# Query weights: conversions of pieces 6 and 7 moved ahead of copies, lower parts moved ahead of the first dots

## What is computed

```python
def peer_ffn(xn, w_query, subkeys, u_tab, v_tab):
    q = (xt @ w_query).reshape(T, PEER_HEADS, 2, PEER_QDIM // 2)
    s = jnp.einsum('thpd,hpkd->thpk', q, subkeys)
    sv, si = lax.top_k(s, PEER_TOPK)
    ...
    top_s, pos = lax.top_k(cand, PEER_TOPK)
    expert = jnp.take_along_axis(cand_id, pos, axis=-1)
    gate = jax.nn.softmax(top_s, axis=-1)
    ...
        act = jax.nn.gelu(jnp.einsum('thkd,td->thk', u_tab[ec], xc), approximate=False)
        return jnp.einsum('thk,thkd->td', gc * act, v_tab[ec])
```

## Time and profile before

| | |
|---|---|
| median of 3 runs | 1543.56 us (1541.64 to 1547.15) |
| profiled execution | 1545.37 us, of which 1543.6 us are the span of the trace |
| TensorE busy | 1382.1 us (90%) |
| VectorE busy | 1030.1 us (67%) |
| ScalarE busy | 710.3 us (46%) |
| GpSimd busy | 562.7 us (36%) |
| DMA | 414.99 MB, mean 269 GB/s |

### The profile page before, as it was taken

One profiled execution on the slowest core, in us unless ns is written; L12 is line 12 of the kernel. 1 busy time (PEld: TensorE's weight loads), 2 busy tenths in 40 slices (PEclk: granted clock), 3 DMA queues, 4 the chain that ended last, 5 costly groups with the idle time before them and its releaser, 6 DMA issues.

```text
span 1543.6 us, 18198 instructions
## 1 busy us (share of the span) xinstructions
PE 1382.1 (90%) x5969; PEld 969.5 (63%) x5969; DVE 1030.1 (67%) x1918; ACT 710.3 (46%) x1377; POOL 562.7 (36%) x537
## 2 busy tenths in 40 slices
PE   7999998778877877787888999999999999999998
PEld 5887963333333332333335878788888778888887
DVE  5885687666666666666655548569863586498734
ACT  5545553322223333322324463377645755776534
POOL 3031454333333433333342422045443512364414
PEclk9999999999999899999898999899999999999999
DMA  9295699999999999999997510557664443476650
GB/s 314 92 181 184 248 389 421 421 422 421 422 422 422 421 422 422 421 422 421 422 420 274 191 51 10 164 165 216 190 218 175 163 139 104 126 208 194 215 190 28
DMA packets 180739, 414.99 MB, mean 269 GB/s; under 512 B 9178, under 2 KB 113218, under 8 KB 148418
## 3 DMA queue, kind: packets, MB, share of 16 engines
q0 software_dynamic: 37440, 268.45, 41.9%
q1 hardware_dynamic: 143090, 145.66, 30.7%
q10 hardware_dynamic: 144, 0.04, 0.0%
HBM read 409.93 MB, written 4.19 MB: 268 GB/s over the span
## 4 chain that ended last, share of the span: by engine, by line
PE 52%; DMA 24%; DVE 8%; ACT 6%; POOL 5%; issue 4%; ACTq 0%; POOLq 0%; DVEq 0%
DMA expert_rows<-in_peer_uv,route_idx 16%; PE ps L2515 9%; PE ps L2062 8%; PE ps L2064 8%; PE ps L2063 8%; PE ps L2346 8%; DMA work_b<-in_peer_uv,route_idx 6%; PE ps L2516 5%; POOL expert_rows L637 2%; POOL weights_lo L588 2%; DVE weights_lo L440 2%; DMA work_b<-in_peer_u,route_idx 2%; ACT weights_hi L433 2%; PE ps L2027 1%; POOL ple_proj_lo L588 1%
## 5 line engine op out<-in xcount | busy, mean ns | idle before, releaser
L1643 DVE CUSTOM_DVE_ANT_0 expert_rows<-expert_rows,ps 128x1024 f32<-128x1024 f32 x180 | 219.5, 1220 | 134.6 <-DMA expert_rows<-in_peer_uv,route_idx 133.3
L2346 PE MATMUL ps<-expert_rows,proj 128*128 128x512 f32 x512 | 247.6, 641 | 61.6 <-ACT proj L951 61.6
L637 POOL DMA_INDIRECT expert_rows<-in_peer_uv,route_idx x191 | 182.9, 958 | 285.1 <-PE ps L2346 215.1
L588 POOL TENSOR_TENSOR weights_lo<-weights_raw,weights_hi 128x512 fp32r<-128x512 f32 x112 | 147.1, 1348 | 365.7 <-ACT weights_hi L433 291.6
L433 ACT CAST weights_hi<-weights_raw 128x2048 fp32r<-128x2048 f32 x98 | 185.4, 1916 | 104.9 <-PE ps L2064 84.9
L2346 PEld LDWEIGHTS ps<-expert_rows,proj 128*128 128x128 f32 x512 | 102.6, 205 | 205.7 <-issue 122.1
L2515 PE MATMUL ps<-x_normT,weights_hi 128*128 128x512 f32 x640 | 222.5, 392 | 0.0
L440 DVE TENSOR_TENSOR weights_lo<-weights_raw,weights_hi 128x2048 fp32r<-128x2048 f32 x70 | 165.1, 2367 | 64.0 <-ACT weights_hi L433 63.6
L937 ACT ACTIVATE proj<-proj 128x4 f32<-128x4 f32 x64 | 13.1, 205 | 411.5 <-DVE proj L1643 411.5
L2062 PE MATMUL ps<-weights_hi,x_normT 128*128 128x512 f32 (+1 forms) x496 | 189.9, 383 | 12.6 <-DVE weights_lo L440 6.5
L2064 PE MATMUL ps<-weights_hi,x_normT 128*128 128x512 f32 (+1 forms) x496 | 186.6, 376 | 0.0
(11 more groups left out here) (367 smaller groups left out, 2407.1 us busy)
## 6 DMA issues: line engine op xcount, KB each, us to landing
weights_raw<-in_ffn_up SPq DMA_DIRECT2D x88, 512.0 KB, 5.0
weights_raw<-in_ffn_down SPq DMA_DIRECT2D x22, 1024.0 KB, 4.9
weights_raw<-in_ab_w_in SPq DMA_DIRECT2D x14, 1024.0 KB, 5.2
weights_raw<-in_w_in SPq DMA_DIRECT2D x12, 1024.0 KB, 7.9
weights_raw<-in_ple_gate SPq DMA_DIRECT2D x8, 1024.0 KB, 6.7
weights_raw<-in_c_w_in SPq DMA_DIRECT2D x6, 1024.0 KB, 5.7
weights_raw<-in_w_out SPq DMA_DIRECT2D x4, 1024.0 KB, 11.9
weights_raw<-in_peer_w_query SPq DMA_DIRECT2D x4, 1024.0 KB, 11.9
```

The source lines that it names most:

```text
L588: ins = pool.tensor_tensor(w.lo[:, c], w.raw[:, c], w.hi[:, c].bitcast(F32), ALU.subtract)
L637: nc.gpsimd.indirect_dma_start(out=dst, out_offset=None, in_=table, in_offset=bass.IndirectOffsetOnAxis(ap=r_idx[:, q, n:n + 1], axis=0)). ...
L1643: ins = nc.vector.tensor_tensor_reduce(out=rows, in0=rows, in1=tokens, scale=1.0, scalar=0.0, op0=ALU.mult, op1=ALU.add, accum_out=r_dot[: ...
L2346: ins = pe.matmul(PS[:, (J[f"peer_{t}"] + m) % 8, :], DIAG[b][:, k, :], rows[:, m * BANK:(m + 1) * BANK], start=False, stop=False, skip_gr ...
```

## The change

ScalarE's list: the conversion of piece 6 goes ahead of the copy of product 3, and that of piece 7 ahead of the copies of products 4 and 5. VectorE's list: the lower parts of pieces 6 and 7 go ahead of the first block's dots.

```diff
@@ scalar
             query_cols(1)
             query_cols(0)
-            for n in range(4, 8):
+            split("query", 4)
+            query_cols(2)
+            for n in range(5, 7):
                 split("query", n)
-                query_cols(n - 2)
+            query_cols(3)
+            split("query", 7)
+            for m in range(4, 6):
+                query_cols(m)
             weights(0, 0, 0)
             diag(0, 0, wait=False)
             query_cols(6)
@@ vector
-            for n in range(4, 6):
+            for n in range(4, 8):
                 split_lo(v, "query", n)
             v.wait_ge(sem("tokens_scaled"), 1)
             first_dots(0)
-            for n in range(6, 8):
-                split_lo(v, "query", n)
             route_stages(1, 1, range(14))
             first_dots(1)
```

## The result

| | before | changed |
|---|---|---|
| median of 20 runs | 1545.49 us (1541.14 to 1547.66) | 1549.34 us (1547.71 to 1550.93) |
| profiled execution | 1545.37 us, span 1543.6 | 1550.93 us, span 1549.1 |

The ratio is 1.0027, with a 95% interval of 1.0019 to 1.0035. The medians differ by 3.85 us where +2.2 was forecast. The point estimate is inside the 0.3% that count as no change, but the interval is clear of 1. Part of the distance to 1545.8 is the base: the three runs shown before had a median of 1543.56, the twenty have 1545.49. The profiled execution of the changed kernel was the slowest of its twenty.

What follows compares the result with a forecast made beforehand. From about 197 to 820 us a DMA stream of 1 MB gathers was taken to set the time. Score delay 2.6 plus clock 1.7 less free slip 2.1 gave +2.2 us, 1545.8 from 1543.56; range 1541.5 to 1549.0.

Steps and rivals of the forecast that it cites:

- ScalarE: moved, but not earlier: Conversions of pieces 6 and 7 still wait for TensorE's products and stay at 184.85 and 190.61 us; price 0.
- VectorE's lower parts: Piece 6's lower part and gather 6 come 1.1 us sooner, piece 7's and gather 7 stay; gain 0, at best 1.1.
- The dots of block 0: On VectorE they move to 194.82 to 199.4 us, later work slips 4.6 us, VectorE catches up; cost nothing.
- What waits for those dots: ScalarE's weights and copies 6 and 7 wait; scores, gather 13 and unit 1's first gather come 2.6 us later.
- The clock: TensorE's gap among the scores may bring slow matmuls costing 0, 1.7 or 2.9 us more; 1.7 taken.
- What of it reaches the stream: Unit 1's first gather can be issued 2.1 us later for nothing, since the queue was full; sum +2.2 us.
- An unknown: gathers issued under dots: Gather 7 and unit 1's first gather, issued on GpSimd beside VectorE's dots, may each take nothing or 1.0 us longer.
- Gather 13 has more room and does not come into it: Gather 13, moved from 208.56 to 211.2 us, was held to add nothing to the stream's delay.

Runs made afterwards that it cites:

- e1: The kernel before with only ScalarE's half of the change, VectorE as before: 1546.28 us, ratio 1.0003.
- e2: The kernel before with only VectorE's half of the change, ScalarE as before: 1549.19 us, ratio 1.0025.
- e3: The changed kernel, but ScalarE copies products 6 and 7 ahead of block 0's weights: 1545.61 us, ratio 1.0000 to the kernel before.
- e4_slip24: The kernel before with 24 small unread copies on ScalarE ahead of the copy of product 7: 1547.21 us, ratio 1.0009.
- e8: The changed kernel without the four zero matmuls that open the first half's sums: 1546.55 us, ratio 1.0014 to the kernel before.
- e6: Changed kernel with unit 1's routing ahead of block 0's dots on VectorE, and block 0's weights later on ScalarE: 1544.62 us, 0.9987 to the kernel before.
- e9: Changed kernel with copies 6 and 7 ahead of block 0's weights, gather 8 early, no zero matmuls before the first sum: 1544.97 us, 0.9995 to the kernel before.
- r_before: The kernel before, unchanged, run once more for a second trace: ratio 1.0006.
- r_after: The changed kernel run once more for a second trace: ratio 1.0025 to the kernel before.
- e7b: Repeat of e7, the same kernel: 1541.96 us, ratio 0.9986 to the kernel before.
- e5: The kernel before with gather 8 issued ahead of gathers 6 and 7: 1546.67 us, ratio 1.0005.
- the three e4: The kernel before with 12, 17 or 24 small unread copies on ScalarE ahead of the copy of product 7: 1543.70, 1545.07 and 1547.21 us.
- e7: The kernel before with gather 8 issued early and without the four zero matmuls that open the first half's sums: 1542.87 us, ratio 0.9990.

## Why the prediction was wrong

Point by point, by its own steps.

- **ScalarE: moved, but not earlier** was right: conversions in place, e1 1.0003.
- **VectorE's lower parts** was right: gather 6 at 191.08 (189.95 without the 1.13; forecast 189.9), gather 7 at 27.59 us behind the first gather, 27.56 before.
- **The dots of block 0** was right on VectorE: 195.97 less 1.13 is 194.84. That it could catch up was right as well, though its last dot is 1.3 us later than before, since gather 15 landed later.
- **What waits for those dots** was right to 0.2 us: gap 2.43 us (forecast 2.6), copy 7 at 205.65 (206.78 less 1.13; forecast 205.8), unit 1's first gather 2.7 us late (forecast 2.6). e2 and e3 show the path.
- **The clock** was taken at 1.7 us. In both profiles of the changed kernel it cost 0. In e2, e4_slip24 and e8 it cost 1.4 to 1.6.
- **The failed step is "What of it reaches the stream"**: "Its issue can therefore slip 7.6 - 5.5 = 2.1 us for nothing". The last dot of unit 1 came 3.5 and 3.3 us later for an issue 2.7 us later, and unit 15's 2.1 and 2.7 us: nothing was free, and without that term the forecast's 2.6 would have stood between the two. With the clock held, the forecast's own sum was 2.6 + 0 - 2.1 = +0.5. That it said +2.2 is owed to a clock term that did not come; two errors of 2 us cancelled.
- **An unknown: gathers issued under dots** was right that they can be lengthened: gather 8 took 1.99 us under block 0's dots, and 0.94 in e6, where no dots run beside it. It cost nothing at gathers 7 and 8 (e3, e9). The Trainium skill (SBUF — State Buffer, section "Who interferes with whom") infers that generating descriptors is not held up by a VectorE instruction with two SBUF inputs. These runs speak against that for this gather: the dots are the one thing that e6 moves away. The gather also reads its row numbers from SBUF (`route_idx`), so whether its reading or its descriptors waited is not shown.

What the prediction did not see is that the hold-up goes either way. The same dot and the same gather 15, a row of VectorE's timeline and one of GpSimd's, in the kernel before and then in r_before:

```profile
212.04 1.21 DVE L1643 CUSTOM_DVE_ANT_0 expert_rows<-expert_rows,x_norm 128x1024 f32<-128x1024 f32 x1
212.08 1.98 POOL L637 DMA_INDIRECT work_b<-in_peer_uv,route_idx  x1 [0.30 <-issue]
```

```profile
212.03 1.29 DVE L1643 CUSTOM_DVE_ANT_0 expert_rows<-expert_rows,x_norm 128x1024 f32<-128x1024 f32 x1
212.07 0.94 POOL L637 DMA_INDIRECT work_b<-in_peer_uv,route_idx  x1 [0.30 <-issue]
```

Either the gather takes 1 us more or the dot 0.08 us more. Of the first twenty gathers in each of the 16 profiles, 32 begin 0.02 to 0.1 us behind the start of such a dot: 25 took 1.97 to 1.99 us beside a dot of 1.21 to 1.23, and 7 took 0.93 to 0.94 us beside a dot of 1.28 to 1.30.

Why the slip was not free: the landing of one gather was taken for the state of the queue. Gather 7's 5.5 us (when it was issued, gather 6 had 1.0 us to go: 190.98 + 5.7) say how soon one gather lands, not when the next ones do. The rows of the kernel before already gave less. Gather 8, 1.25 us behind gather 7, and unit 1's second gather, 1.24 us behind its first, us from issue to landing:

```profile
scratch<-in_peer_uv,route_idx POOLq DMA_INDIRECT x1, 7.5
```

```profile
expert_rows<-in_peer_uv,route_idx POOLq DMA_INDIRECT x1, 8.8
```

At the second landing only 8.8 - 7.5 = 1.3 us are to be had, not 2.1. e4_slip24 bears this out: its second gather took 7.5 us too and landed 3.0 us late (62.5 against 59.6, counted from the first gather), which is 4.29 - 1.3. In r_after the same working gives 1.4 us, and the second gather was 3.1 us late, as late as the first, after 1.3 us at gather 15 (landed at 55.9 against 54.6). So it explains e4_slip24, but only a part of the change. Gather 13 was issued 2.7 us late too, and "Gather 13 has more room and does not come into it" was the second half of the mistake: between gathers 12 and 13 no gather was issued for 6.63 us instead of 3.07, and some 3 us behind gather 13's issue the rate sagged (351 and then 332 GB/s above) while the engines looked busy. That the low rate comes from few gathers in the queue is read from the place of the sags; no run varied the depth of the queue alone.

**What stays open.** The last dot of unit 15 is 2.1 and 2.7 us later, the medians differ by 3.85. The remainder of 1.1 to 1.8 us is not in the expert units. Of the 5.5 us between the two spans (1543.6 and 1549.1) 1.1 lie ahead of the first gather and 2.3 behind the units, of the 4.6 us between the two repeats 1.4 and 0.5. Profiles of one and the same kernel differ in these places too. The clearest case is e7b against e9, 965 to 975 us, columns as above:

```profile
965.00:975.00 10.00, 9.97 (x60) 7.23 (x60) 8.90 (x10) 4.30 (x6) 0.00 (x0) 1.00 1.12 345
```

```profile
965.00:975.00 10.00, 10.00 (x44) 6.29 (x44) 6.45 (x6) 2.22 (x3) 0.00 (x0) 0.57 1.10 343
```

At clock 1.00 TensorE ran 60 matmuls, at 0.57 only 44. Such a stretch of about 10 us near 970 us is in 8 of the 16 profiles (before, r_before, e1, e3, e5, e8, e9, r_after) and absent in the others (changed, e2, e6, the three e4, e7, e7b). The changed kernel has it in one profile and not in the other, so it is no fixed property of a kernel. Six of the eight without it have a last column of 718 to 720. The other two do not: e2 has 722.1, and the changed kernel 724.7 with another stretch of low clock near 1208 us. Why only one of 28 runs of the changed kernel was under 1547.7 us (1546.02, in r_after) while the kernel before reached 1541.1 is thus not settled by the profiles. The lower medians of e6, of the e4 kernels and of e8 belong to the same open question.

## What to carry to other kernels

Before a step is moved ahead of another on an in-order engine, look at what stands behind the *next* engine's wait for the other: here the price was gone once two copies queued on ScalarE behind a wait for dots were moved ahead of it. Where a stage is a stream, count the time of each issue against the stream, not the landing of one transfer, and read GB/s beside the busy share. A transfer brought forward may pay only if the next unit's transfers are issued sooner as well, as e5 and e7 suggest.

## What the runs showed of the hardware

- The DMA engines were 94 to 97% busy at 332 to 351 GB/s, where gathers of the same kind moved 419 to 428 GB/s at a share of 1.01 to 1.02. This was seen where gathers had been issued late.
- Gathers 7 and 8 took 1.16 to 1.99 us to issue while VectorE ran dots that read both operands from SBUF (0.94 us once, in e8), and 0.93 to 0.94 us at the same place without them. In two profiles of one kernel either the gather was long (1.98 us, dot 1.21) or the dot (1.29 us, gather 0.94).
- Behind equal gaps of 2.4 to 2.5 us TensorE kept 2.4 GHz in two profiles and fell to 1.2 GHz for a part of the next 40 matmuls in three (4.73 against 6.16 to 6.36 us).
- About 10 us at half the clock behind the units are there in some executions of a kernel and not in others. Two kernels that reached that point alike ended 3.7 us apart.
